# Retention, latent attention and cross attention re-ordered around the weight panels in a one-core Trainium2 program

## The reference

```python
# retention (4 heads, key 256, value 512, two directions), with layer norm
q, k, v, g = split(x @ w_in)                      # 1024 -> 6144 columns
q, k = rotary(q), rotary(k) / 16
y = (q k^T * decay) v                             # per head, both directions
out = (silu(g) * group_norm(y)) @ w_out           # 2048 -> 1024
# peer0: product-key experts, 128 x 128 of them, u and v streamed from memory
# mla: latent attention (8 heads, 128 + 64 rotary)
c_q, c_kv, k_rope = split(x @ w_in)               # 384, 256, 64 columns
q = rms_norm(c_q) @ w_uq;  k_nope, v = split(rms_norm(c_kv) @ w_ukv)
p = softmax((q_nope k_nope^T + q_rope k_rope^T) * scale);  out = (p v) @ w_out
# peer1: as peer0
# mixers: pooling, RWKV-7 recurrence, differential attention, then @ w_out
# cross: attention of 4 heads of 256 to a memory of 256 rows
q = rms(h_n @ wq) * q_norm;  k = rms(mem_n @ wk) * k_norm;  v = mem_n @ wv
h = h + (softmax(q k^T / 16) v) @ wo
# ffn
h = h + (gelu(conv3(a)) * b) @ w_down             # (a, b) = h_n @ w_up, 2 x 2816
```

## Time and profile before

| | |
|---|---|
| median of 3 runs | 2812.56 us (2802.19 to 2814.07) |
| time of the profiled execution | 2816.6 us |
| its span in the trace | 2814.7 us |
| TensorE's mean granted clock | 0.945 of full |
| PE, DVE, ACT busy | 89%, 77%, 33% of the span |

### The profile page before, as it was taken

How to read it: one execution, slowest core, us unless ns; L and a number is a source line. 1 busy time by engine, 2 the same in 40 slices (tenths; PEclk the granted TensorE clock), 3 DMA queues, 4 the chain that set the end, 5 groups by cost and what they waited for, 6 DMA issues and landing times.

```text
span 2814.7 us, 41236 instructions
## 1 busy us (share of the span) xinstructions
PE 2514.0 (89%) x16382; PEld 2256.4 (80%) x16382; DVE 2159.0 (77%) x3186; ACT 915.7 (33%) x1403; POOL 293.5 (10%) x122
## 2 busy tenths in 40 slices
PE   5987999999999999576999999999997888666988
PEld 5866998999988887545998999988886777555987
DVE  6767897999866667746897999867767655785987
ACT  1000244444445554010244444454444442000000
POOL 0000297000000000000396000000000010000000
PEclk9998999999999999767999999999999998888999
DMA  5633577666677776312576666677775430431554
GB/s 176 181 118 112 163 213 207 180 185 188 201 245 255 241 243 215 91 54 67 184 214 198 188 181 185 213 254 245 243 242 182 128 100 10 136 120 53 171 166 136
DMA packets 201711, 484.41 MB, mean 172 GB/s; under 512 B 23984, under 2 KB 93872, under 8 KB 201008
## 3 DMA queue, kind: packets, MB, share of 16 engines
q1 hardware_dynamic: 197360, 471.37, 54.2%
q10 hardware_dynamic: 4160, 10.40, 1.1%
HBM read 447.08 MB, written 34.60 MB: 171 GB/s over the span
## 4 chain that ended last, share of the span: by engine, by line
PE 56%; DVE 31%; POOL 5%; DMA 4%; issue 2%; ACT 2%; ACTq 0%; DVEq 0%; SPq 0%
PE psum L992 24%; PE psum L787 20%; DVE rounded L1401 8%; DVE halves L2220 7%; DVE halves L2217 5%; PE psum L945 5%; POOL rounded L760 5%; DMA sb<-in_u_turned 2%; DVE rounded L1397 2%; PE psum L1100 1%; ACT rounded L2548 1%; DVE sb L1436 1%; PE psum L1068 1%; PE psum L1070 1%; PE psum L831 1%
## 5 line engine op out<-in xcount | busy, mean ns | idle before, releaser
L1401 DVE TENSOR_TENSOR rounded<-sb,rounded 128x1024 fp32r<-128x1024 f32 (+3 forms) x696 | 812.7, 1172 | 273.9 <-ACT rounded L2548 233.5
L787 PE MATMUL psum<-rounded 128*128 128x256 f32 (+1 forms) x4380 | 729.5, 329 | 83.8 <-DVE rounded L1401 43.3
L2548 ACT ACTIVATE rounded<-sb 128x1024 fp32r<-128x1024 f32 x512 | 542.8, 1060 | 790.1 <-PE psum L992 327.3
L945 PE MATMUL psum<-rounded 128*128 128x256 f32 x6144 | 773.8, 285 | 14.0 <-POOL rounded L760 13.9
L787 PEld LDWEIGHTS psum<-rounded 128*128 128x128 f32 x4380 | 654.1, 197 | 158.7 <-DVE rounded L1401 36.4
L945 PEld LDWEIGHTS psum<-rounded 128*128 128x128 f32 x6144 | 746.7, 192 | 17.7 <-POOL rounded L760 17.7
L992 PE MATMUL psum<-rounded,weights 128*128 128x512 f32 x3072 | 697.3, 389 | 0.4 <-ACT sb L2564 0.4
L992 PEld LDWEIGHTS psum<-rounded,weights 128*128 128x128 f32 x3072 | 576.3, 188 | 120.7 <-issue 1.2
L760 POOL TENSOR_TENSOR rounded<-sb,rounded 128x1024 fp32r<-128x1024 f32 x96 | 267.9, 2806 | 1256.0 <-ACT rounded L2548 1255.5
L1397 DVE CAST rounded<-sb 128x1024 fp32r<-128x1024 f32 (+3 forms) x263 | 169.2, 644 | 112.6 <-PE psum L787 96.5
L2220 DVE TENSOR_TENSOR halves<-halves,small 128x1536 bf16<-128x1536 bf16 x128 | 225.0, 1758 | 4.4
(11 more groups left out here) (326 smaller groups left out, 1352.1 us busy)
## 6 DMA issues: line engine op xcount, KB each, us to landing
sb<-in_u_turned SPq DMA_DIRECT2D x256, 512.0 KB, 4.0
sb<-in_peer_v SPq DMA_DIRECT2D x256, 512.0 KB, 3.5
hidden<-sb SPq DMA_DIRECT2D x256, 128.0 KB, 4.0
sb<-hidden SPq DMA_DIRECT2D x256, 128.0 KB, 3.4
sb<-in_ret_w_in SPq DMA_DIRECT2D x48, 512.0 KB, 4.2
sb<-in_ffn_w_up SPq DMA_DIRECT2D x40, 512.0 KB, 4.3
sb<-in_peer_w_q SPq DMA_DIRECT2D x32, 512.0 KB, 3.8
sb<-in_ffn_w_down SPq DMA_DIRECT2D x22, 512.0 KB, 4.1
```

Source lines behind the costliest of these rows:

```text
L787: mm = pe.matmul(o, a[p], b[q], start=(first and i == 0), stop=(last and i == 2), skip_group_check=True)
L945: mm = pe.matmul(ps(bank, 1)[:, 0:T], u[p][:, k * P:(k + 1) * P], hT[:, q, k, :], start=(k == 0 and w == 0), stop=(k == KD - 1 and w == 2))
L1401: vec.tensor_tensor(ring_lo[0:k, part, 0:wide], ring[0:k, slot, 0:wide], ring_hi[0:k, part, 0:wide].bitcast(F32), ALU.subtract).then_inc(c ...
L2548: act.activation(ring_hi[:, n % SPLIT, :], ring[:, n % RING, :], ACT.Copy).then_inc(tile_hi, 1)
```

## The change

Three stages are re-ordered, and ScalarE takes the high part of more weights. By part:

- **Casts to ScalarE.** `BY_ACT` now also holds ret_in0 to 5, ret_out, the four cross matrices, up0 to 5 and down: 64 + 32 + 70 chunks. `hi_to(...)` calls are written into `act_retention`, `act_cross` and `act_ffn`; VectorE keeps `lower` for them.
- **Start.** The first transposes wait for x and the identity only (`x_loaded`), and retention's first steps for four parameters (`early_loaded`), in place of all.
- **Retention.** Scores follow ret_in3; the product with v for the first 128 tokens runs inside panel ret_in4 (before its chunk 2), for the others after it. The gate is applied by halves; the transposes of y run inside ret_in5 (chunk 6) and ret_out (chunk 5). A second operand buffer `hT2` takes the first half.
- **Latent attention.** Rotary angles are worked out in peer0's second half (`mla_angles`). ScalarE squares and sums mla_in from PSUM. All 64 score matmuls of the eight heads run first, with a signal after each 16; the maximum, Exp (with bias and running sum, from PSUM) and the division go in four parts; the transposes and products follow.
- **Cross attention.** The memory is loaded, normalised, transposed and split inside mixers and panel mix_out. Panels in the order wk, wq, wv, wo. q is kept unnormalised: q's gain is multiplied into k's, and its sum of squares is made by 32 matmuls against ones (2 columns each) and enters through Exp's scale. Softmax runs beside panel wv.
- **Feed-forward.** The hidden values are split after each up panel (`hid_split`), and panel down waits for each group of four chunks by itself.

```diff
-BY_ACT = ("slots0", "slots1", "slots2", "slots3", "diff_v", "pool_in", "mix_out")
+BY_ACT = ("ret_in0", "ret_in1", "ret_in2", "ret_in3", "ret_in4", "ret_in5", "ret_out",
+          "slots0", "slots1", "slots2", "slots3", "diff_v", "pool_in", "mix_out",
+          "xa_wk_2", "xa_wq_2", "xa_wv_2", "xa_wo_2", "up0", "up1", "up2", "up3", "up4", "up5", "down")
...
+                def first_heads(k):
+                    if k == 2:
+                        pe.wait_ge(*decayed)
+                        pe.wait_ge(*v_ready)
+                        heads(0)
...
+                panel("ret_in4", hk, "tokens", 0, 1024, between=first_heads)
+                silu_done[0] = banks.lend(range(4), "a")
+                heads(1)
+                hold(range(4))
+                panel("ret_in5", hk, "tokens", 0, 1024, between=first_half)
+                silu_done[1] = banks.lend(range(4), "a")
+                hold(range(4, 8))
+                panel("ret_out", lambda k: split_of(hT2 if k < KD else hT)(k % KD), "tokens", 4, D, fed=0, between=second_half)
...
-                    pe.wait_ge(*banks.lend(range(4), "v"))
-                    hold(range(4, 8))
-                    wait_all(turn_p(a["p"], 4))
...
+                        mm.then_inc(psum_for_vec, 1)
+                back = []
+                for n in range(2):
+                    pe.wait_ge(vec_for_pe, to_pe.up(TB))
+                    back.append(turn_p(a["p"][n], 4 * n))
...
+                    if k == 3:
+                        pe.wait_ge(*vec_told.of("mn"))
+                        turn_mem(0, 6)
...
+                        turn_mem(1, 4)
...
+                panel("xa_wk_2", hm, "tokens", 4, D, between=turn_x)
...
+                panel("xa_wq_2", hk, "features", 0, 8, streamed=True, between=turn_k)
...
+                panel("xa_wv_2", hm, "tokens", 0, D, between=turn_shares)
...
-                panel("down", four_by_four, "tokens", 4, D, fed=0)
+                panel("down", split_of(hid_split), "tokens", 4, D, fed=0)
...
+                    if b > 3:
+                        tb = b - 4
+                        if tb == 0:
+                            vec.wait_ge(mem_loaded, 16)
+                        moments(a["mem"], tb)
...
+                    if n == 2:
+                        hi_to(begin[key] + 6)
+                        root(rstd[:, 0:4])
+                    if n == 3:
+                        hi_to(begin[key] + 4)
+                        root(rstd[:, 4:8])
+                    hi_to(end[key] + 2)
+                    act.wait_ge(chunks_done, end[key])
...
+                    for tb in range(TB):
+                        act.wait_ge(vec_for_act, from_vec.up())
+                        for i in range(4):
+                            act.activation(a["p"][n][:, tb, i, :], ps(4 * n + 2 * tb + i // 2, 1)[:, (i % 2) * T:(i % 2 + 1) * T], ACT.Exp,
+                                           scale=MLA_SCALE, bias=a["top"][:, n, tb, i:i + 1], accum_out=a["sum"][:, n, tb, i:i + 1]
+                                           ).then_inc(*(own.mark(act_for_vec) if i == 3 else own.next()))
...
+                hi_to(wq + 3)
+                in_place(a["ksum"].rearrange("p b h -> p (b h)"), ACT.Sqrt)
+                hi_to(wq + 7)
+                act.wait_ge(psum_for_act, psum_a.up())
...
                     w = min(4, FF_TILES - 4 * n)
-                    in_place(a["conv"][:, n % 2, 0:w, :].rearrange("p a b -> p (a b)"), ACT.Gelu)
+                    hi_to(end[f"up{n}"] + 4)
+                    act.wait_ge(vec_for_act, from_vec.up())
+                    v = a["conv"][:, n % 2, 0:w, :].rearrange("p a b -> p (a b)")
+                    act.activation(v, v, ACT.Gelu).then_inc(*own.mark(act_for_vec))
+                hi_to(end["down"])
```

More of the change, by code:

```diff
@@ L91 @@
 TURN_AFTER = 44
+ANGLES_AT = 128 + 64
 FIRST_GROUP = 47
@@ new lines, in pe_cross @@
+                wait_all(values)
+                for half in range(2):
+                    for i in range(4 * half, 4 * half + 4):
+                        for kb in range(TB):
+                            mm = pe.matmul(ps(4 + i // 2, 1)[:, (i % 2) * T:(i % 2 + 1) * T],
+                                           a["v"][:, kb, i * P:(i + 1) * P], a["pT"][:, i // 2, kb, :],
+                                           start=(i % 2 == 0 and kb == 0), stop=(kb == 1), skip_group_check=True)
+                    mm.then_inc(psum_for_act, 1)
+                    banks.lend([4 + 2 * half, 5 + 2 * half], "v")
@@ L2090, in vec_cross @@
-                from_psum()
-                take_split(hT[:, 0], hT[:, 1], 4, 4)
+                for tb in range(TB):
+                    moments(h, tb)
+                    r, mean = rstd[:, tb:tb + 1], mv[:, tb, 0:1]
+                    vec.tensor_tensor(r, mean, mean, ALU.mult).then_inc(*own.next())
+                    done()
+                    vec.scalar_tensor_tensor(r, r, RMS_EPS, mv[:, tb, 1:2], ALU.add, ALU.add).then_inc(*own.mark(vec_for_act))
+                    more(1, "xa_wk_2")
@@ new lines, in vec_cross @@
+                for tb in range(TB):
+                    inverse_root(tb)
+                    vec.tensor_scalar(a["hn"][:, tb, :], h[:, tb, :], rstd[:, tb:tb + 1], None, ALU.mult).then_inc(*own.mark(vec_for_pe))
+                    more(1, "xa_wk_2")
+                vec.memset(a["ones"], 1.0).then_inc(*own.next())
+                split_to(begin["xa_wk_2"] + 6)
+                take_columns("xa_wq_2", norm_col("xa_norm_g_2", 0))
+                split_to(end["xa_wk_2"] + 2)
+                vec.wait_ge(params_loaded, loads[phase])
@@ new lines, in vec_cross @@
+                done()
+                top = flat8(a["top"])
+                vec.scalar_tensor_tensor(top, top, -1.0, qinv, ALU.mult, ALU.mult).then_inc(*own.mark(vec_for_act))
+                more(1, "xa_wv_2")
+                for tb in range(TB):
+                    total = a["sum"][:, tb, :]
+                    vec.wait_ge(act_for_vec, from_act.up())
+                    vec.reciprocal(total, total).then_inc(*own.next())
+                    done()
+                    for i in range(XH):
+                        v = a["p"][:, tb, i, :]
+                        vec.tensor_scalar(v, v, total[:, i:i + 1], None, ALU.mult).then_inc(
+                            *(own.mark(vec_for_pe) if i == XH - 1 else own.next()))
+                    more(1, "xa_wv_2")
@@ new lines, in act_cross @@
+                act.activation(a["qT"][:, 4:8, :].rearrange("p a b -> p (a b)"), ps(2, 2), ACT.Copy).then_inc(*own.mark(act_served))
+                sq = a["sq"].rearrange("p b d -> p (b d)")
+                qT = a["qT"].rearrange("p a b -> p (a b)")
+                done()
+                act.wait_ge(*q_taken[0])
+                for half in range(2):
+                    act.activation(sq[:, half * 1024:(half + 1) * 1024], qT[:, half * 1024:(half + 1) * 1024], ACT.Square).then_inc(
+                        *(own.mark(act_for_pe) if half else own.next()))
@@ L2595, in act_peer @@
                         load_params(phase)
+                    if i == ANGLES_AT + 2 and phase == "peer0":
+                        mla = A["mla"]
+                        act.wait_ge(vec_for_act, from_vec.up())
+                        act.activation(mla["cos"], mla["cos"], ACT.Sin).then_inc(*own.next())
+                        act.activation(mla["sin"], mla["sin"], ACT.Sin).then_inc(*own.mark(act_for_vec))
+                ahead.n = end[phase + "_v"]
                 if phase == "peer1":
```

542 lines of the change are left out of this document (352 added, 190 removed), and 2 rows, old and new, of the table PE_TOLD.

## The result

| | before | after |
|---|---|---|
| median | 2808.59 us, 4 runs | 2675.86 us, 4 runs (2675.09 to 2680.68) |
| profiled execution | 2816.6 us | 2675.7 us |
| its span | 2814.7 us | 2673.8 us |
| TensorE's mean granted clock | 0.945 | 0.965 |

The ratio is 0.9532, 95% interval 0.9505 to 0.9559: faster, by 132.7 us in the medians. 2665 was forecast, with a range of 2630 to 2712.

A forecast was written before the change was run, and what follows sets the result against it. TensorE, busy 89%, was taken as the bound, its idle time mostly ended by VectorE. Terms 38 + 13 + 28 + 57 + 13 - 1 = 148 us off 2816.6 give 2668.6, median 2665, range 2630 to 2712.

The forecast's parts named there:

- Retention: Start to ret_out's end: re-ordering removes TensorE's waits, end near 234 instead of 272.1; 38 us saved, bounds 30 and 46.
- Latent attention, first part: mla_in to first transposes: angles, copy and squares leave VectorE, loads about 1 us earlier; 13 us saved (8 to 15).
- Latent attention, second part: First score to mla_out: scores without pause, 35 us, softmax mostly below them; 28 us saved, bounds 20 and 43.
- rival B: Latent attention's scores run at the full clock, 20 us instead of 35; time 2650, chance 0.13.
- check of 0.80: Sign named ahead: in the windows by stage, the clock of latent and cross attention stands above 0.80.
- Cross attention: Memory work inside mixers, softmax beside wv, wo starting at 2513 instead of 2568.7; 57 us saved (47 to 64).
- Feed-forward: Wait ahead of panel down goes, up5 stalls about 6 us against 4 before; 13 us saved (6 to 15).
- Peer0: Takes latent attention's angles, some 4 us of VectorE where it has slack; 1 us lost (0 to 2).
- Casts: 166 chunks lose 0.69 us each on VectorE, 115 us; nothing by itself, but it makes the other parts possible.
- C: Casts stand in ScalarE's order behind waits, some 20 places of 2.5 us; 50 us given back, 2715, chance 0.19.
- D: Cast, low part and matmuls come in series, up to 2.3 us more per chunk; slower, 3045, chance 0.04.
- E: No change: transfers set the pace and idle time returns behind the weights' loads; 2805, chance 0.04.

The follow-up runs named there:

- experiment 4: Changed kernel with ScalarE issuing latent attention's two gains ahead of the two 1024-column norm parameters: 2668.7 us, ratio 0.9502.
- padded kernel: Changed kernel with latent attention's rotary operands filled with zeros from 64 to 128 rows: 2656.1 us, ratio 0.9452.
- Experiment 3: Changed kernel with one more VectorE split beside feed-forward's convolution and ScalarE's cast for it ahead of Gelu: 2665.8 us; with the cast alone 2674.0.
- casts alone: Kernel before, with only the 166 chunks' casts moved to ScalarE: 2809.3 us, ratio 0.9992.
- grouped one: Changed kernel with each part's four 128-row score matmuls first, then its four of 64 rows: 2658.2 us, ratio 0.9453.
- first version put together: Changed kernel with grouped scores, both feed-forward edits, gains first, earlier casts in retention and peer0's angles in three pieces: 2640.0 us, ratio 0.9393.
- order alone: Changed kernel with the casts of retention, cross attention and feed-forward back on VectorE: 2698.8 us, ratio 0.9603.

## Why the prediction was right, and where not

The order of the work was read rightly, and the waits that were to go went; the sum of 148 was 7 us too high. Nearly all of that is one mis-sized term, feed-forward (8.5 us), and smaller errors of either sign cancel. The profiled execution was forecast at 2668.6 and took 2675.7. The other 4 us of the miss in the median come from the allowance for how far the profiled execution of before lay above the median.

- **Retention**, 38 forecast, 38.8 measured: ret_out ends at 233.3, not 234. The stalls named are there (1.87, 1.82, 1.59), each in the place named. That the sum came out so close is partly luck: from the first chunk on TensorE is idle for 9.0 us where 14 were counted, and its work takes 206.3 us where 201.8 were. The first four chunks alone take 2.7 us more than priced, at a granted clock of 0.51 up to 24 us.
- **Latent attention, first part**, 13 forecast, 11.2 measured. The step that failed is that the last load would land 1 us earlier with two loads fewer. It was issued 1.4 us earlier, counted from mla_in's start, but VectorE could start 9.3 us after its issue instead of 7.0, and so 0.9 us later. In both kernels it stood behind 2 x 1024 columns, which experiment 4 shows to cost 4 to 5 us; where the extra 2.3 us come from is not shown. The idle time ahead of the transposes is 12.55, just above the 12 of the check.
- **Latent attention, second part**, 28 forecast, 31.2 measured. The scores took 35.2 us as forecast from the earlier trace rows, and rival B fell for this kernel; 14.3 us from the last score to mla_out where 16 were counted. Rows 8 gave the right price without its reason. The rule of the Trainium skill that was weighed there (TensorE: Matmul & The Clock Gate, its table of the two states) goes against the trace in this kernel, if busy is what the profile counts as busy: 0.50 from 1167.4 to 1200.7 without idle time. It agrees with the trace where all rows are 128: 1.00 from 1166 to 1182 in the padded kernel. The window's clock of 0.77 missed the check of 0.80.
- **Cross attention**, 57 forecast, 58.0 measured. wk to wo took 103.1 us against 103.6 worked out; the ones matmuls 4.2 against 6 taken; wk starts right behind mix_out. No later wait took the place of the softmax. Here too two errors cancel: mix_out to wk saved 25.6 us where 22.8 were worked out, and 2.1 us were lost ahead of mix_out. The working had counted 2 us for the memory's moments and 3.9 for its transposes, but 2409.5 adds only 4 to mix_out's old end.
- **Feed-forward**, 13 forecast, 4.5 measured, below the lower bound of 6. This is the mis-sized term. The wait ahead of down went as said (12.51 us before, 0.79 after), and down gained 2.4. But the forecast looked only at up5 for what the moved splitting costs, and took up0 to up4 as unchanged. There the split that stood between tap 0 and Gelu before now stands behind the product, and each panel takes 24.49 us instead of 192 x 108.24/900 = 23.09: 5.6 us in four panels, and 7.2 us over the 996 matmuls from up0's start to the end of the piece before the 1.29 us. That is 3.06 us a chunk instead of 2.89, one of the signs that the forecast had named against itself. Experiment 3 gets back 8.8 us between up0 and down.
- **Peer0**, -1 forecast with bounds 0 to 2, -2.4 measured. The 4 us of VectorE were right (914.61 to 918.53), but in one piece they outlast the slack of one step: 1.29 us of idle time right behind them. With the angles in pieces the stage, from its first panel's start to mla_in's, is 849.7 and 848.8 us long in two profiles, beside 849.0 before and 851.4 in the changed kernel. The 1.1 us beyond the idle time were not traced to a place; profiles in which the angles stand in one piece differ by 1.3 us here (850.4 to 851.6).
- **Casts**. "None of it counts by itself" held: no change that can be measured. That it makes the other parts possible was too strong: the order without the casts already gives some 110 of 133 us.
- **Rivals.** C, ScalarE's order as the wait, is right in kind and small: 1.87 and 1.82 us in retention, not 20 places of 2.5. D finds nothing: casts alone are no slower than before. Nor does E: ScalarE's casts do wait for weights at times, up to 3.8 us in feed-forward, but the new idle time there went with the edits of experiment 3, which leave the loads as they are.

## What to carry to other kernels

When idle time ahead of a panel is removed by spreading work over earlier panels, go through each of them and write down the gap between two splits in VectorE's order, not only the sum of its work: here closing a gap of 5.35 us in each up panel was worth 8.8 us, where the wait that went was one of 12.5. A queue of loads at a stage's start should begin with the one that is waited for first. Moving work off an engine is worth nothing where it lay beside the bound, and worth something only once a new order puts other work there.

## What the runs showed of the hardware

- A change between matmuls of 128 rows and of 64 rows (float32, 256 columns) costs 0.19 us at the upper level of the clock and 0.29 at the lower, whether it comes after every second record or after every eighth. At such a change no weight load runs for 0.33 us at the upper level and 0.65 at the lower (the changed kernel, the grouped one and the first version put together). The 64-row matmuls themselves take as long as the 128-row ones: 1.92 us for eight of either in the grouped kernel. Operands filled with zeros to 128 rows avoid the change.
- With a change after every second record, the clock stays at the lower level although the profile shows TensorE busy throughout: in the changed kernel the granted clock is 0.97 from 1165.5 to 1167.4 and 0.50 from there to 1200.7. Five profiles with this order (the changed kernel, order alone, gains first, both feed-forward kernels) agree within 0.01 us in the median matmul of 128 rows (0.63 us). With 128 rows throughout, it is at the full clock in two profiles and falls for 3.4 us in the third.
- How long the clock stays down when the two shapes come in fours differs from one kernel to the next: 3.4 us in one profile, some 17 us in the other, and what sets it is not settled.
- A load's time from issue to landing depends on what was issued ahead of it: the same gain of 256 columns could be used 9.3 us after its issue behind 2 x 1024 columns, and 5.2 us after it when it was issued ahead of them. Behind 2 x 1024 columns it was 7.0 us in the kernel before, so the figure varies.
